# A two-layer encoder step on one core: the chunk loop of the delta-rule mixer written out as a software pipeline, and a third raw buffer for an expert table

## The chip, the core and the metric

The kernel runs on one core of one Trainium2 chip. The metric is device microseconds of one execution, the median of several runs. TensorE (PE in the profile), VectorE (DVE), ScalarE (ACT), GpSimdE (POOL) and SyncE (SP, which here only issues DMAs) each run their own list of instructions in order and meet through semaphores.

## The reference

Two streams, a prompt of 512 positions and a decode of 32, go through two layers in float32. The part of a layer that the change touches most is the RWKV-7 group, a recurrence over time on a 64x64 matrix state for each of eight heads:

```python
def step(S, inp):
    r_t, w_t, k_t, v_t, a_t, b_t = inp
    sa = jnp.einsum('bhij,bhj->bhi', S, a_t)
    S = S * w_t[:, :, None, :] + sa[..., None] * b_t[:, :, None, :] + v_t[..., None] * k_t[:, :, None, :]
    return S, jnp.einsum('bhij,bhj->bhi', S, r_t)
```

A layer also has an RG-LRU group (convolution and a scan), an output projection, a PEER expert layer, and a per-layer embedding. In the expert layer each of 8 heads picks 16 of 16,384 experts by product keys; `hid = xb . u[e]` and `out = sum gelu(hid) gate v[e]`. The outputs are the activations and the states after each stream. Prompt and decode have states of their own: the prompt's starts at zero, the decode's is an input.

## The kernel before

The two layers run one after the other, each as a chain of stages: input projection with the RG-LRU work inside it, RWKV preparation, **the chunk loop**, output projection, query projection, **the u phase** of the expert layer, its v phase, embedding.

**The chunk loop.** The recurrence is done in chunks of C = 64 positions: eight of the prompt and one (DEC0, 32 positions padded) of the decode, NCHUNK = 9. A chunk turns the recurrence into matrix products. TensorE makes the products of the scaled keys `s.bk` and queries `s.ar` (`products`, L733 ff., 8 matmuls, then 8 transposes through `ident`); DVE masks them (`first`, `second`); the triangular system is inverted by doubling in six levels (`level_y` L749, `level_x` L758 on TensorE, one ACT copy `s.ys` between them, and a mask and an add on DVE for each level); `right_side` (L773) applies the incoming state `st`; `finish` (L785) solves, makes the state's update and the outputs; DVE's `carry` (L1601) adds the update into `st` and decays it. Each group of eight matmuls appears as 16 records of 64x64x64 in the trace. Everything of a chunk that does not read `st` is independent of the chunk before it.

Two slots (`Slot(0)`, `Slot(1)`) hold the buffers and four PSUM banks each. A hardware loop (`Fori`, four passes) takes two neighbouring chunks at a time, and both slots go through the same step at about the same time: products of slot 0 and slot 1, then level by level 0, 1, 0, 1. Slot 0's right side is placed after level 1, slot 1's only after slot 0's `finish` and `carry`, for it needs the state. Only when both carries are done are the `tilde` operations for the next two chunks run on DVE (L1561). The decode chunk is run last, alone, after the loop; DVE first saves the prompt's state to `stp` and puts the decode's state into `st`. `passed` adds a semaphore increment behind most waits.

**The u phase.** 128 tiles of the u table (`in_ut`, 512 KB each) are loaded by SP in two halves (`load_u`, L499) into one of two raw buffers `uraw`. ACT copies a half to a rounded high part `uh` (`high_u`, L1190), DVE subtracts to the low part `ul` (`low_u`, L1790), and `hidden` (L873) on TensorE multiplies high and low parts with the activations. SP waits before a load until DVE has read the same half two tiles earlier (`ul_ready`). In DVE's list the tiles are taken in 64 pairs: 8 head pairs, then three blocks of ten `route` pairs (top-k, many DVE operations) and eight `hot` pairs (one-hot gate matrices), then two pairs. Between them go row gathers by POOL, their dot products on DVE (`weigh_row`, L1806), saves of the activations (`expert_inputs`) and of the gate matrix by ACT's DMA queue.

**Constants.** `cn` holds constants in SBUF for the whole run, loaded once: identity, masks, then `eye` (64 columns), `level` (384), `reset` (580) and `fold`.

Of the kernel before, what the change touches and what calls it, by code (L numbers as in the profile page):

```python
# [85 lines left out]
NUG = 5  # L86
NV = 4
# [3 lines left out]
assert PART <= PAIRS_U and HOT_PAIRS * 4 == GB  # L91

# [57 lines left out]
def trunk(nc, x, p, small, const, spread, mixw, wkv0, w_in, w_out, wq, keys, ut, u, v, wple, y, small_out, wkv_out):  # L150
    ctx = ExitStack()
    with ctx:
# [30 lines left out]
        sm = take(NSM)  # L183
        cn = take(NCN)
# [51 lines left out]
        class Slot:  # L236


            def __init__(self, i):
# [4 lines left out]
                self.ar = take(NT * P).rearrange("p (m t) -> p m t", m=NT)  # L244
# [40 lines left out]
        uraw = [take(KD * P).rearrange("p (k n) -> p k n", k=KD) for _ in range(2)]  # L285
        uh_at = aligned(top[0])
# [84 lines left out]
        nsp_ready = sem("nsp_ready")  # L371
# [13 lines left out]
        state_ready = sem("state_ready")  # L385
# [19 lines left out]
        u_in = [[sem(f"u_in{i}{half}") for half in range(2)] for i in range(2)]  # L405
# [13 lines left out]
        eos_out, accg_out = sem("eos_out"), sem("accg_out")  # L419
# [12 lines left out]
        waits_passed = {e.engine: sem(f"waits_passed{i}") for i, e in enumerate([nc.sync, nc.tensor, nc.vector, nc.scalar])}  # L432

# [6 lines left out]
        def passed(eng):  # L440


            eng.sem_inc(waits_passed[eng.engine], 1)
# [12 lines left out]
        def _(sp_):  # L456
# [17 lines left out]
            for L in range(DEPTH):  # L474
# [43 lines left out]
                for m in range(2, NK):  # L518
# [96 lines left out]
        def _(pe):  # L615
# [53 lines left out]
            for L in range(DEPTH):  # L669
# [59 lines left out]
                pe.wait_ge(cum_ready, L + 1)  # L729

                def products(s, k):
# [8 lines left out]
                    last.then_inc(s.pair_done, 1)  # L740
                    for m in range(NT):
                        nc.tensor.transpose(ps[:, s.bank + 2, m * P:(m + 1) * P], s.bk[:, m, :], ident)
# [4 lines left out]
                def level_y(s, k, lv):  # L747

                    n = L * s.per + k  # L749
                    if lv == 0:  # L750
                        pe.wait_ge(s.turn_out, n + 1)
                    pe.wait_ge(s.m_ready, n * (LEVELS + 1) + lv + 1)
                    passed(pe)
# [5 lines left out]
                def level_x(s, k, lv):  # L759
                    pe.wait_ge(s.y_out, (L * s.per + k) * (LEVELS - 1) + lv)  # L760
                    passed(pe)
# [9 lines left out]
                def right_side(s, k):  # L771

                    pe.wait_ge(s.gm_ready, L * s.per + k + 1)  # L773
                    if s.i == 1:
                        pe.wait_ge(state_ready, L * s.per + k + 1)
                    passed(pe)
                    for m, q in PAIRS:
                        hd = 2 * m + q // HD
                        mm(s.psum(0)[q:q + C, m, :], s.ar[:, m, 0:C], st[:, m, q:q + HD], start=True, stop=False)
# [4 lines left out]
                def finish(s, k):  # L784
# [4 lines left out]
                    passed(pe)  # L789
# [3 lines left out]
                    pe.wait_ge(s.sa_out, n + 1)  # L793
                    passed(pe)
# [4 lines left out]
                    for m in range(NT):  # L799
                        mm(s.psum(0)[:, m, :], st[:, m, :], s.ar[:, m, C:P], start=True, stop=False)  # L800
# [6 lines left out]
                def chunks(k, work):  # L807

                    for s in work:
                        products(s, k)  # L810
                    for lv in range(LEVELS):
                        for s in work:
                            level_y(s, k, lv)
                        if lv > 0:
                            for s in work:
                                level_x(s, k, lv)
                        if lv == 1:
                            right_side(slots[0], k)
                    for s in work:
                        if s.i == 1:  # L820
                            right_side(s, k)
                        finish(s, k)

                passed(pe)
# [140 lines left out]
                pe.wait_ge(accg_out, L + 1)  # L965
                back(acc_g, 6)
                for t in range(NB):
                    pe.wait_ge(eos_out, L * NB + t + 1)
                    back(eos[t], 2 * t)
# [27 lines left out]
        def _(act):  # L997
# [28 lines left out]
            for L in range(DEPTH):  # L1026
# [13 lines left out]
                act.wait_ge(lam_step, 2 * L + 1)  # L1040
# [6 lines left out]
                def lru_tanh(ns):  # L1047
                    act.wait_ge(nsp_ready, L + 1)
# [15 lines left out]
                for n in range(2, IN_T):  # L1064
                    high_weight(L, 0, n, wh1)
                    if n == 2:
                        act.wait_ge(lam_step, 2 * L + 2)
# [52 lines left out]
                def values(s, col):  # L1120

# [3 lines left out]
                def turned(s, k):  # L1125
                    act.wait_ge(s.turn_done, L * s.per + k + 1)
                    av(s.bkT, ps[:, s.bank + 2, :], ACT.Copy)
                    av(s.sav, ps[:, s.bank + 3, :], ACT.Copy).then_inc(s.turn_out, 1)

                def level(s, k, lv):  # L1130
# [3 lines left out]
                def right_side(s, k):  # L1134
# [3 lines left out]
                def finish(s, k, col):  # L1138
                    n = L * s.per + k
                    act.wait_ge(s.sa_done, n + 1)  # L1140
# [4 lines left out]
                    act.wait_ge(s.step_done, n + 1)  # L1145
                    passed(act)
                    av(o[:, :, col], s.psum(0), ACT.Copy).then_inc(o_out, 1)

                def chunks(k, work, col):
                    for s in work:  # L1150
                        values(s, col(s))
                    for s in work:
                        turned(s, k)
                    for lv in range(1, LEVELS):
                        for s in work:
                            level(s, k, lv)
                        if lv == 1:
                            right_side(slots[0], k)
                    for s in work:
                        if s.i == 1:  # L1160
                            right_side(s, k)
                        finish(s, k, col(s))

                with act.Fori(0, NCH // 2) as k:
                    chunks(k, slots, lambda s: bass.ds(k * (2 * C) + s.i * C, C))
                chunks(NCH // 2, slots[:1], lambda s: slice(DEC0, DEC0 + C))
# [24 lines left out]
                def high_u(m, half):  # L1191
                    i = L * NK + m
                    act.wait_ge(u_in[m % 2][half], 16 * (i // 2 + 1))
# [808 lines left out]
```

## Time and profile before

| | |
|---|---|
| median of 3 runs | 4164.2 us (4155.7 to 4173.1) |
| the profiled execution | 4173.6 us, of which the span in the trace is 4171.8 us |
| mean granted TensorE clock | 0.933 of full |
| PE busy | 3686.5 us (88%) |
| DVE busy | 2972.4 us (71%) |
| ACT, POOL busy | 1655.2 us (40%), 922.7 us (22%) |
| chunk loop, layer 0 and layer 1 | 216.5 to 455 us, 2289 to 2523.5 us |
| u phase, layer 0 | about 665 to 1447 us |
| v phase, layer 0 | about 1453 to 1987 us |

Busy time is instruction time of an engine; matmuls are pipelined, and a busy PE isn't at its peak. The clock column of a window is the TensorE clock granted, where 1.00 is 2.4 GHz and 0.50 is 1.2 GHz. In the chain of waits each row is a start, a length and the work that the end of the run waited for in that time; "issue" is time for which the profile shows nothing, often a semaphore on its way.

### The profile page before, as it was taken

Reading aid. Unit: us, or ns where it says so; the run is one execution under the profiler, and the core shown is the slowest. Engines: PE = TensorE matmul, PEld = TensorE weight load, DVE = VectorE, ACT = ScalarE, POOL = GpSimd, SP = SyncE. Lnnn points to the kernel's source line nnn. Section 1 sums busy time; section 2 is a strip of 40 time slices with the busy share of each in tenths; the row PEclk is TensorE's granted clock in tenths of the full one; section 3 lists DMA queues with packets and bytes.
Section 4 is the critical chain, followed back from the end, with each engine's and each line's share of the span. In section 5 each row is a group of like instructions: output and inputs, shape, how many; then the busy total and the mean of one; then the engine's idle time right before and its main releaser. Section 6 shows DMA issues by size and latency. Waiting matters only on the chain.

```text
span 4171.8 us, 65717 instructions
## 1 busy us (share of the span) xinstructions
PE 3686.5 (88%) x24642; PEld 3310.0 (79%) x24642; DVE 2972.4 (71%) x6046; ACT 1655.2 (40%) x3067; POOL 922.7 (22%) x742
## 2 busy tenths in 40 slices
PE   8877798889898799999888777979998997999998
PEld 8766597889898688888787666978888886888877
DVE  5845325988989598888367542279898895888882
ACT  4312022366666633333233210223847575333331
POOL 3200031222222233333031000302222232333320
PEclk9977799999999899999999877999999998999999
DMA  3100023669898999998221000247798989999972
GB/s 119 50 1 0 19 81 129 233 232 314 280 310 282 296 394 380 379 380 330 75 80 42 1 0 28 82 136 251 255 322 268 313 270 319 390 379 380 380 279 64
DMA packets 544480, 888.94 MB, mean 213 GB/s; under 512 B 37808, under 2 KB 361936, under 8 KB 543440
## 3 DMA queue, kind: packets, MB, share of 16 engines
q1 hardware_dynamic: 311728, 444.32, 30.3%
q0 software_dynamic: 92416, 336.17, 23.1%
q10 hardware_dynamic: 140064, 104.88, 7.9%
q8 instruction: 164, 2.69, 0.3%
q14 instruction: 108, 0.88, 0.1%
HBM read 777.55 MB, written 107.67 MB: 212 GB/s over the span
## 4 chain that ended last, share of the span: by engine, by line
PE 62%; DVE 21%; DMA 5%; ACT 5%; issue 3%; ACTq 2%; DVEq 2%; SPq 0%
PE ps L955 26%; PE ps L647 10%; PE ps L631 7%; PE ps L879 5%; DMA m<-in_ut 4%; DVE m L1795 3%; PE ps L916 3%; DVE m L1806 3%; PE ps L882 2%; ACT m L1231 1%; ACTq L1249 1%; DMA expert_inputs<-m 1%; PE ps L623 1%; PE ps L755 1%; PE ps L763 1%
## 5 line engine op out<-in xcount | busy, mean ns | idle before, releaser
L955 PE MATMUL ps<-m,m 128*128 128x512 f32 x4608 | 1066.9, 394 | 11.9 <-DVE m L1867 11.9
L955 PEld LDWEIGHTS ps<-m,m 128*128 128x128 f32 x4608 | 867.2, 188 | 211.3 <-issue 12.4
L879 PE MATMUL ps<-m,m 128*128 128x384 f32 x4096 | 846.5, 349 | 53.6 <-ACT m L1204 53.1
L879 PEld LDWEIGHTS ps<-m,m 128*128 128x128 f32 x4096 | 737.6, 196 | 58.6 <-ACT m L1204 56.8
L608 POOL DMA_INDIRECT m<-in_u,m x320 | 352.2, 1101 | 1128.3 <-DVE m L1806 927.3
L882 PE MATMUL ps<-m,m 128*128 128x384 f32 x2048 | 465.0, 350 | 135.4 <-DVE m L1795 135.1
L1197 ACT ACTIVATE m<-m 128x512 fp32r<-128x512 f32 x512 | 319.3, 625 | 590.9 <-DMA m<-in_ut 473.3
L608 POOL DMA_INDIRECT m<-in_v,m x320 | 359.5, 1124 | 786.0 <-DVE ps L1879 554.0
L1303 ACT ACTIVATE m<-m 128x1024 fp32r<-128x1024 f32 x256 | 271.5, 1061 | 651.3 <-PE ps L955 648.1
L882 PEld LDWEIGHTS ps<-m,m 128*128 128x128 f32 x2048 | 376.6, 197 | 155.2 <-DVE m L1795 155.2
L647 PE MATMUL ps<-m,m 128*128 128x272 f32 x3648 | 469.0, 290 | 5.5 <-ACT m L1021 4.6
L647 PEld LDWEIGHTS ps<-m,m 128*128 128x128 f32 x3648 | 463.6, 190 | 9.0 <-issue 5.4
L1795 DVE TENSOR_TENSOR m<-m,m 128x512 fp32r<-128x512 f32 x512 | 332.9, 688 | 96.6 <-ACT m L1197 94.4
L580 POOL TENSOR_TENSOR m<-m,m 128x1024 fp32r<-128x1024 f32 x76 | 191.6, 2523 | 629.9 <-ACT m L1021 629.9
L1879 DVE SCALAR_TENSOR_TENSOR ps<-m,m,ps 128x1024 f32<-128x1024 f32 x254 | 326.2, 1284 | 4.6
L1852 DVE TENSOR_TENSOR m<-m,m 128x1024 fp32r<-128x1024 f32 x256 | 312.1, 1219 | 14.3 <-ACT m L1303 14.3
L1806 DVE CUSTOM_DVE_ANT_0 m<-m,ps 128x1024 f32<-128x1024 f32 x256 | 306.4, 1217 | 6.5 <-issue 0.5
L631 PE MATMUL ps<-m,m 128*128 128x272 f32 x1152 | 275.1, 401 | 39.2 <-DVE m L1664 20.6
L631 PEld LDWEIGHTS ps<-m,m 128*128 128x128 f32 x1152 | 223.6, 195 | 87.5 <-DVE m L1664 21.5
L1817 DVE TENSOR_SCALAR m<-m,m 128x128 f32<-128x128 f32 x768 | 213.2, 348 | 79.2 <-PE ps L916 56.4
L1231 ACT ACTIVATE m<-m,m 128x128 f32<-128x128 f32 x768 | 243.8, 392 | 0.5
L916 PE MATMUL ps<-m,m 128*128 128x128 f32 x1536 | 207.4, 278 | 17.7 <-DVE m L1817 13.8
(264 smaller groups left out, 4009.5 us busy)
## 6 DMA issues: line engine op xcount, KB each, us to landing
m<-in_ut SPq DMA_DIRECT2D x512, 256.0 KB, 5.1
m<-in_v SPq DMA_DIRECT2D x256, 512.0 KB, 6.3
expert_inputs<-m ACTq DMA_DIRECT2D x256, 192.0 KB, 3.7
gate_matrix<-m ACTq DMA_DIRECT2D x48, 1024.0 KB, 9.7
m<-gate_matrix SPq DMA_DIRECT2D x256, 192.0 KB, 5.2
m<-expert_inputs SPq DMA_DIRECT2D x256, 192.0 KB, 7.2
m<-in_w_in SPq DMA_DIRECT2D x44, 512.0 KB, 3.8
m<-in_wq SPq DMA_DIRECT2D x32, 512.0 KB, 3.9
```

The lines of the kernel that those rows point to most:

```text
L608: pool.indirect_dma_start(ug[r % NUG], None, table[:, :], bass.IndirectOffsetOnAxis(ap=index.bitcast(U32), axis=0)).then_inc(row_in[r % NU ...
L631: last = mm(ps[:, bank + a, 0:HALF], wslot[:, slot, k, :], rhs[:, n, a * HALF:(a + 1) * HALF], start=(n == 0), stop=(n == len(ks) - 1))
L647: last = mm(ps[:, 2 * j + a, 0:HALF], lhs[j][:, k, :], rhs[:, k, a * HALF:(a + 1) * HALF], start=(k + w == 0), stop=(k == KD - 1 and w == 2))
L879: mm(ps[:, j, 0:DT], uh[j][:, k, :], x_[:, k, :], start=(k == 0 and x_ is xh), stop=False)
L882: last = mm(ps[:, j, 0:DT], ul[j][:, k, :], xh[:, k, :], start=False, stop=(k == KD - 1))
L916: last = mm(ps[:, 4 + s, j * P:(j + 1) * P], oneA[:, s, j, :], oneB[:, s, j, :], start=True, stop=True)
L955: last = mm(ps[:, 2 * t + a, :], lhs[s][:, t * BLK:(t + 1) * BLK], rhs[s][:, a * 512:(a + 1) * 512], start=(n + w == 0), stop=(n == NK - 1 ...
L1197: av(uh[m % 2][:, ks, :], uraw[m % 2][:, ks, :], ACT.Copy).then_inc(uh_ready, 1)
L1795: tt(ul[m % 2][:, ks, :], uraw[m % 2][:, ks, :], uh[m % 2][:, ks, :].bitcast(F32), ALU.subtract).then_inc(ul_ready, 1)
L1806: nc.vector.tensor_tensor_reduce(row, row, other, 1.0, 0.0, ALU.mult, ALU.add, at).then_inc(row_used, 1)
L1852: tt(vl[n % NV], vraw[n % NV], vh[n % NV].bitcast(F32), ALU.subtract).then_inc(vl_ready, 1)
L1879: last = stt(acc, row, w, acc, ALU.mult, ALU.add)
```

## The change

The two `Fori` loops on TensorE, ACT and DVE are gone. All nine chunks are written out, p = 0 to 8, with p = 0 the decode chunk; chunk p uses slot p % 2. One step of the written-out loop holds the first half of chunk p ("new") and the second half of chunk p - 1 ("old"), interleaved group by group. `products` is cut into `pairs`, `turn_keys` and `turn_values`; `finish` into `solve` and `step`; `tilde` into `tilde_keys` and `tilde`. The queries `s.ar` get a second buffer per slot (in the place of the mixer weights `mw`). `carry(p - 2)` opens DVE's step p. The `tilde` work for chunk p + 1 is in step p. `pairs` and `right_side` wait for two different semaphores of the carry: `state_read` after its PSUM reads and `state_ready` at its end. The decode's state is put into `st` before the loop; after `carry(0)` it is saved to `sts` and `st` is cleared.

```diff
-                passed(pe)
-                with pe.Fori(0, NCH // 2) as k:
-                    chunks(k, slots)
-                chunks(NCH // 2, slots[:1])
...
+                def pairs(p):
+                    s, k = turn_of(p)
                     n = L * s.per + k
                     pe.wait_ge(s.tilde_ready, n + 1)
-                    pe.wait_ge(s.v_ready, n + 1)
-                    passed(pe)
+                    if p > 1:
+                        pe.wait_ge(state_read, L * NCHUNK + p - 1)
+                        pe.wait_ge(o_out, L * NCHUNK + p - 1)
                     for m, q in PAIRS:
-                        last = mm(ps[:, s.bank + q // HD, m * P:(m + 1) * P], s.bk[q:q + HD, m, :], s.ar[q:q + HD, m, :],
+                        last = mm(ps[:, s.bank + q // HD, m * P:(m + 1) * P], s.bk[q:q + HD, m, :], s.ar[k % 2][q:q + HD, m, :],
                                   start=True, stop=True)
                     last.then_inc(s.pair_done, 1)
...
+                for p in range(NCHUNK + 1):
+                    new, old = p < NCHUNK, p > 0
+                    if new:
+                        pairs(p)
+                    if old:
+                        level_y(p - 1, 3)
+                    if new:
+                        turn_keys(p)
+                    if old:
+                        level_x(p - 1, 3)
+                    if new:
+                        turn_values(p)
+                    if old:
+                        level_y(p - 1, 4)
+                        right_side(p - 1)
+                        level_x(p - 1, 4)
+                    if new:
+                        level_y(p, 0)
+                    if old:
+                        level_y(p - 1, 5)
+                    if new:
+                        level_y(p, 1)
+                    if old:
+                        level_x(p - 1, 5)
+                    if new:
+                        level_x(p, 1)
+                    if old:
+                        solve(p - 1)
+                    if new:
+                        level_y(p, 2)
+                    if old:
+                        step(p - 1)
+                    if new:
+                        level_x(p, 2)
...
+                def carry(p):
+                    s, k = turn_of(p)
+                    end = cols_of(p).stop - 1
                     dve.wait_ge(s.step_done, L * s.per + k + 1)
                     for q in (0, HD):
                         at = st[q:q + HD, :, q:q + HD]
-                        tt(at, s.psum(1)[q:q + HD], at, ALU.add)
+                        last = tt(at, s.psum(1)[q:q + HD], at, ALU.add)
+                    last.then_inc(state_read, 1)
                     dve.drain()
                     for q in (0, HD):
                         at = st[q:q + HD, :, q:q + HD]
-                        tt(at, at, TB[1][q:q + HD, :, end].to_broadcast([HD, NT, HD]), ALU.mult)
-                    dve.drain()
-
-                def chunks(k, work, col, end):
-                    for s in work:
-                        tilde(s, col(s))
-                    for s in work:
-                        first(s, k)
-                    for s in work:
-                        second(s, k)
-                    dve.drain()
-                    for lv in range(1, LEVELS):
-                        for s in work:
-                            level(s, k, lv)
-                    for s in work:
-                        carry(s, k, end(s))
-                        if s.i == 0 and len(work) == 2:
-                            dve.sem_inc(state_ready, 1)
-
-                with dve.Fori(0, NCH // 2) as k:
-                    chunks(k, slots, lambda s: bass.ds(k * (2 * C) + s.i * C, C),
-                           lambda s: bass.ds(k * (2 * C) + (s.i * C + C - 1), 1))
-                dve.wait_ge(wkv_in, L * 16 + 16)
+                        last = tt(at, at, TB[1][q:q + HD, :, end:end + 1].to_broadcast([HD, NT, HD]), ALU.mult)
+                    if p == 0:
+                        dve.drain()
+                        for q in (0, HD):
+                            copy(sts[q:q + HD, :, :], st[q:q + HD, :, q:q + HD])
+                        dve.drain()
+                        last = dve.memset(st[:, :, :], 0.0)
+                    last.then_inc(state_ready, 1)
+                    dve.drain()
...
+                for p in range(NCHUNK + 1):
+                    new, old = p < NCHUNK, p > 0
+                    if p > 1:
+                        carry(p - 2)
+                    if new:
+                        first(p)
+                    if old:
+                        level(p - 1, 3)
+                    if new:
+                        first_inverse(p)
+                    if old:
+                        level(p - 1, 4)
+                    if new:
+                        second(p)
+                    if p + 1 < NCHUNK:
+                        tilde_keys(p + 1)
+                    if old:
+                        level(p - 1, 5)
+                    if new:
+                        level(p, 1)
+                        masked(p)
+                    if p + 1 < NCHUNK:
+                        tilde(p + 1)
+                    if new:
+                        level(p, 2)
+                carry(NCHUNK - 1)
...
+                for p in range(NCHUNK + 1):
+                    new, old = p < NCHUNK, p > 0
+                    if old:
+                        level(p - 1, 3)
+                    if new:
+                        turned_keys(p)
+                    if old:
+                        level(p - 1, 4)
+                    if new:
+                        turned_values(p)
+                    if old:
+                        right_side(p - 1)
+                    if p + 1 < NCHUNK:
+                        values(p + 1)
+                    if old:
+                        level(p - 1, 5)
+                    if new:
+                        level(p, 1)
+                    if old:
+                        solved(p - 1)
+                    if new:
+                        level(p, 2)
+                    if old:
+                        stepped(p - 1)
```

Of the three loops the first is TensorE's, the second DVE's, the third ACT's. On DVE `tilde_keys(0)` and `tilde(0)` come before the loop and `carry(NCHUNK - 1)` after it.

The u phase gets NU = 3 raw buffers. The third lies over `eye`, `level` and `reset` of `cn`; SP loads these constants again at the start of layer 0's v phase, and DVE and TensorE wait for them in layer 1.

```diff
-                        if m > 1:
-                            sp_.wait_ge(ul_ready, 2 * (i - 2) + half + 1)
-                        sp_.dma_start(uraw[m % 2][:, ks, :], ut[L, m][:, ks, :]).then_inc(u_in[m % 2][half], 16)
+                        if m >= NU:
+                            sp_.wait_ge(ul_ready, 2 * (i - NU) + half + 1)
+                        sp_.dma_start(uraw[m % NU][:, ks, :], ut[L, m][:, ks, :]).then_inc(u_in[m % NU][half], 16)
...
+                load_u(2)
+                for m in range(3, NK):
...
                 load_v(0)
                 load_v(1)
+                if L + 1 < DEPTH:
+                    back = slice(CN["eye"], CN["eye"] + D)
+                    sp_.dma_start(cn[:, back], const[:, back]).then_inc(const_in, 16)
```

`passed` and its semaphores are dropped, and a few semaphores are joined (`nsp_ready` into `lam_step`, `accg_out` and `eos_out` into `sums_out`), with the same order of work.

## Rows read from the trace of the kernel before

**Rows 1.** The page: the span, and the shares of the chain that ended last.
```profile
span 4171.8 us, 65717 instructions
...
PE 62%; DVE 21%; DMA 5%; ACT 5%; issue 3%; ACTq 2%; DVEq 2%; SPq 0%
```

**Rows 2.** Windows over both chunk loops: us, busy us of engines (instructions), clock, DMA, GB/s.
```profile
216.46:455.00 238.54, 172.45 (x3169) 152.37 (x3169) 112.07 (x253) 47.89 (x114) 0.00 (x0) 0.74 0.00 1
2289.00:2523.50 234.50, 169.17 (x3169) 149.69 (x3169) 111.58 (x253) 47.89 (x114) 0.00 (x0) 0.76 0.00 1
```

**Rows 3.** Chain of waits, first two chunks of layer 0: start us, us, what.
```profile
221.58 2.08 PE ps L738 x16
...
225.55 1.12 PE ps L738 x16
...
242.41 0.68 PE ps L755 x16
243.09 0.47 PE ps L763 x16
...
244.92 1.11 issue
...
249.04 0.52 PE ps L791 x16
...
250.50 0.69 PE ps L797 x16
...
254.26 2.07 issue
...
261.06 1.12 PE ps L797 x16
...
266.36 0.42 DVE m L1606
...
271.18 2.08 PE ps L738 x16
```

**Rows 4.** Chain of waits, the decode chunk of layer 0, alone.
```profile
416.29 2.08 PE ps L738 x16
...
432.42 1.13 PE ps L755 x16
...
434.10 1.12 PE ps L763 x16
...
454.90 7.17 PE ps L655 x16
```

**Rows 5.** Groups by line on DVE, chunk loop of layer 0: busy us, mean ns | idle before.
```profile
L1597 DVE TENSOR_TENSOR m<-ps,m 128x512 f32<-128x512 f32 x36 | 24.8, 689 | 36.3 <-PE ps L767 35.9
L1571 DVE TENSOR_TENSOR m<-m,m 128x256 f32<-128x256 f32 x54 | 22.6, 419 | 1.1
...
L1606 DVE TENSOR_TENSOR m<-ps,m 64x256 f32<-64x256 f32 x18 | 7.6, 422 | 65.4 <-PE ps L803 65.3
```

**Rows 6.** Windows of 2 us around the first two chunks.
```profile
252.00:254.00 2.00, 2.00 (x18) 1.56 (x17) 0.00 (x0) 0.00 (x0) 0.00 (x0) 0.70 0.00 0
254.00:256.00 2.00, 0.26 (x4) 0.07 (x2) 1.49 (x4) 0.38 (x1) 0.00 (x0) 0.50 0.00 0
...
276.00:278.00 2.00, 2.00 (x22) 1.72 (x21) 0.88 (x3) 0.28 (x1) 0.00 (x0) 0.83 0.00 0
```

**Rows 7.** A window of 10 us in the second pass of the loop.
```profile
286.00:296.00 10.00, 9.16 (x276) 8.58 (x273) 5.54 (x11) 2.19 (x7) 0.00 (x0) 1.00 0.00 0
```

**Rows 8.** Waits of the whole run: us in total, times, longest us.
```profile
DVE m L1795 <- ACT m L1197: 94.4, 40, 26.8
```

**Rows 9.** Windows over the second route stretch and the hot stretch behind it.
```profile
985.00:1098.00 113.00, 94.60 (x506) 90.91 (x506) 100.76 (x290) 39.36 (x73) 23.63 (x21) 0.95 0.96 316
...
1098.00:1195.00 97.00, 95.13 (x636) 92.86 (x635) 87.18 (x219) 94.78 (x230) 29.62 (x30) 1.00 0.82 271
```

**Rows 10.** The page: DMA issues, KB each, median us to landing.
```profile
m<-in_v SPq DMA_DIRECT2D x256, 512.0 KB, 6.3
```

More of the change, by code:

```diff
@@ L86 @@
 NUG = 5
+NU = 3
 NV = 4
@@ L91, with u_loads @@
 assert PART <= PAIRS_U and HOT_PAIRS * 4 == GB
+def u_loads(L, m):
+    return L * len(range(m % NU, NK, NU)) + m // NU + 1
 def place(p):
@@ L183, in trunk @@
         sm = take(NSM)
+        cn_at = aligned(top[0])
         cn = take(NCN)
@@ L243, in __init__ @@
                 self.bk = take(NT * P).rearrange("p (m t) -> p m t", m=NT)
-                self.ar = take(NT * P).rearrange("p (m t) -> p m t", m=NT)
+                self.ar = [take(NT * P, at).rearrange("p (m t) -> p m t", m=NT) for at in (None, mw_at + i * NT * P)]
                 self.vc = take(NT * P).rearrange("p (m t) -> p m t", m=NT)
@@ L285, in trunk @@
         uraw = [take(KD * P).rearrange("p (k n) -> p k n", k=KD) for _ in range(2)]
+        assert CN["level"] + LEVELS * C == CN["reset"] and MW + LEVELS * C + C >= D
+        uraw.append(take(D, cn_at + CN["eye"]).rearrange("p (k n) -> p k n", k=KD))
         uh_at = aligned(top[0])
@@ L384, in trunk @@
         cum_ready, exp_ready = sem("cum_ready"), sem("exp_ready")
-        state_ready = sem("state_ready")
+        state_read, state_ready = sem("state_read"), sem("state_ready")
         o_out = sem("o_out")
@@ L404, in trunk @@
         gate_saved = [sem(f"gate_saved{i}") for i in range(4)]
-        u_in = [[sem(f"u_in{i}{half}") for half in range(2)] for i in range(2)]
+        u_in = [[sem(f"u_in{i}{half}") for half in range(2)] for i in range(NU)]
         v_in = [sem(f"v_in{i}") for i in range(NV)]
@@ L438, in trunk, with turn_of, cols_of @@
         v_rows = v.rearrange("l e d -> (l e) d")
-        def passed(eng):
-            eng.sem_inc(waits_passed[eng.engine], 1)
+        def turn_of(p):
+            return slots[p % 2], p // 2
+        def cols_of(p):
+            return slice(DEC0, DEC0 + C) if p == 0 else slice((p - 1) * C, p * C)
         def halves(bank, w):
@@ L757, in level_y, with level_x @@
                     last.then_inc(s.y_done, 1)
-                def level_x(s, k, lv):
+                def level_x(p, lv):
+                    s, k = turn_of(p)
                     pe.wait_ge(s.y_out, (L * s.per + k) * (LEVELS - 1) + lv)
-                    passed(pe)
                     for m, q in PAIRS:
@@ L782, in right_side, with solve @@
                     last.then_inc(s.f_done, 1)
-                def finish(s, k):
+                def solve(p):
+                    s, k = turn_of(p)
                     n = L * s.per + k
@@ L792, in finish, with step @@
                     last.then_inc(s.sa_done, 1)
-                    pe.wait_ge(s.sa_out, n + 1)
-                    passed(pe)
+                def step(p):
+                    s, k = turn_of(p)
+                    pe.wait_ge(s.sa_out, L * s.per + k + 1)
                     for m, q in PAIRS:
@@ L1144, in finish, with stepped @@
                     last.then_inc(s.sa_out, 1)
[L1145 to L1149, printed above, removed]
-                    for s in work:
-                        values(s, col(s))
-                    for s in work:
-                        turned(s, k)
-                    for lv in range(1, LEVELS):
-                        for s in work:
-                            level(s, k, lv)
[L1157 to L1166, printed above, removed]
+                def stepped(p):
+                    s, k = turn_of(p)
+                    act.wait_ge(s.step_done, L * s.per + k + 1)
+                    av(o[:, :, cols_of(p)], s.psum(0), ACT.Copy).then_inc(o_out, 1)
+                act.wait_ge(cum_ready, L + 1)
+                values(0)
+                for p in range(NCHUNK + 1):
[22 more added lines that the diff above has]
+                        stepped(p - 1)
                 act.wait_ge(wide_done, wide_of(L, "var"))
@@ L1192, in high_u @@
                     i = L * NK + m
-                    act.wait_ge(u_in[m % 2][half], 16 * (i // 2 + 1))
+                    act.wait_ge(u_in[m % NU][half], 16 * u_loads(L, m))
                     if m > 1:
@@ L1559, in _, with tilde_keys @@
                 eyes = eye.unsqueeze(1).to_broadcast([P, NT, C])
-                def tilde(s, col):
+                def tilde_keys(p):
+                    s, k = turn_of(p)
+                    col = cols_of(p)
+                    if k > 0:
+                        dve.wait_ge(s.turn_done, 2 * (L * s.per + k))
                     for q, (b_at, k_at) in ((0, (0, C)), (HD, (C, 0))):
@@ L1590, in second, with level @@
                     last.then_inc(s.gm_ready, 1)
-                def level(s, k, lv):
+                def level(p, lv):
+                    s, k = turn_of(p)
                     if lv + 1 < LEVELS:
@@ L1599, in level @@
                         tt(s.xt, s.psum(3, NT * C), s.xt, ALU.add).then_inc(s.m_ready, 1)
-                def carry(s, k, end):
+                def carry(p):
+                    s, k = turn_of(p)
+                    end = cols_of(p).stop - 1
                     dve.wait_ge(s.step_done, L * s.per + k + 1)
@@ new lines, in carry @@
+                    last.then_inc(state_ready, 1)
+                    dve.drain()
+                tilde_keys(0)
+                tilde(0)
+                for p in range(NCHUNK + 1):
[23 more added lines that the diff above has]
+                        level(p, 2)
@@ L1633, in _ @@
+                carry(NCHUNK - 1)
                 for q in (0, HD):
                     copy(stp[q:q + HD, :, :], st[q:q + HD, :, q:q + HD])
-                dve.drain()
-                for q in (0, HD):
-                    copy(st[q:q + HD, :, q:q + HD], sts[q:q + HD, :, :])
-                chunks(NCH // 2, slots[:1], lambda s: slice(DEC0, DEC0 + C), lambda s: slice(DEC0 + C - 1, DEC0 + C))
-                for q in (0, HD):
-                    copy(sts[q:q + HD, :, :], st[q:q + HD, :, q:q + HD])
```

123 lines of the change are left out of this document (65 added, 58 removed).

## The prediction

> **What bounds the kernel now.** I read the page's chain first: over the 4171.8 us span PE ends 62% of it and DVE 21% [rows 1], so a stage is worth something only where one of these two, or the way between them, shortens. The profiled execution took 4173.6 us (1.8 around the span), 9.4 over the median of 4164.2; I sum against the former and take 9.4 off at the end.
>
> Then the windows of the stage that is changed. The chunk loop takes 238.5 and 234.5 us, 11% of the span together. No engine fills it: PE 172 busy of 238.5, DVE 112, ACT 48, and PE's clock is 0.74 [rows 2]. So it is bound by hand-offs and by the clock. The chain shows both. In a fast stretch eight matmuls of a level take 0.68 to their end, the next eight are issued 0.47 after the last [rows 3]. One pass of two chunks runs from 221.58 to 271.18, 49.6 us, and its second half is poor: solve, two ACT copies (249.56 to 250.50), step (3.76, to 254.26), 2.07 until the carry is through, and then all again for the other slot at half clock, where a step takes 5.3 (261.06 to 266.36) [rows 3]. The carry, tilde and the next products follow one after the other until 271.18. The decode chunk alone goes from 416.29 to 454.90, 38.6 us [rows 4].
>
> The clock by rows: it is 0.70 in 252 to 254 and 0.50 after it, when PE has been busy 0.26 of 2 us, and 0.83 in 276 to 278 [rows 6]. The first products of a pass run at half clock (2.08), the second slot's, 4.0 us of unbroken matmuls later, at full (1.12) [rows 3]. With two slots level on level PE is busy 9.16 of 10 us and the clock stays at 1.00 [rows 7].
>
> **The chunk loop, step by step.** In the new loop a step holds one chunk's work. I lay it out at full clock from t = 0, where the old chunk's `step` has been issued. `level_x(new, 2)`: 2 x 0.47, done at 1.15. DVE adds it (0.69, [rows 5]): 1.9. Carry's first two operations (2 x 0.42, [rows 5]): 2.8. Only then may `pairs` start, for it waits for `state_read`: 2.95 to 4.05 (1.12, [rows 3]). Behind that wait on PE's queue stand all groups of the next step, level 3 of the older chunk among them, so the wait is a hole of 1.8 us that nothing fills. Then y3 and the four key transposes (half of a pair group, an estimate) to 5.0; x3 waits for ACT's copy, 5.3 to 6.25; value transposes to 6.75; y4 waits for DVE's add, 7.3 to 7.8; right side (16 matmuls, 0.94 and its tail) to 8.95; x4 to 9.9; y0 to 10.4; y5 after mask and add (0.42 + 0.69) 11.0 to 11.5; y1 to 11.95; x5 12.25 to 12.7; x1 to 13.7; solve to 14.2; y2 after DVE's add 14.8 to 15.3, which hides the two ACT copies; step 3.76 to 19.1. DVE's own work in a step (112.07 / 9 = 12.5 us, [rows 2]) fits beside this, and carry's second half, 1.9 to 3.75 in all, is over long before the right side needs the state. `tilde`, gone from the path, lies where DVE waits for PE.
>
> So a step takes **19.1 at full clock**, against 24.8 for a chunk of a pass now. At half clock the same list has 24.4 of PE work (pairs 1.9, transposes 1.7, six y 5.1, x 7.65, right side 1.9, solve 0.85, step 5.3; a group of eight issues in 0.85, 1.12 to its end, [rows 3, 4]) and 2.8 of holes: **27.2**.
>
> Which clock? A step's end is like what it is now: a hole before `step`, then `step`, then 1.8 of nothing, and there the clock fell [rows 6]. Behind `pairs` come 4 us of nearly unbroken work, after which it rose [rows 3]. So I take it low from about 0 to 7 of each step, which adds 0.96 for pairs, 0.4 for y3, 0.35 for transposes, 0.4 for half of x3 and 0.3 at the edges: **21.5**.
>
> The ends: step 0 has only the new chunk, 11 at full and 14 at half clock (416.29 to 432.42 less the right side, [rows 4]): 12.5. Step 1 has no carry to wait for: 19.5. Steps 2 to 8: 7 x 21.5 = 150.5. Saving the decode's state and clearing `st` in step 2: 1.2. The last step has only the old chunk: at half clock 432.42 to 454.90 and the right side, 24.4 with carry and copies [rows 4]; at full 18.2; taken 21.3. Sum 205.0. Now, from first products to the stage's end, it is 233.3 (221.58 to 454.90, [rows 3, 4]), and 229.4 in layer 1 (4 shorter, [rows 2]). That saves 28.3 + 24.4 = **52.7**. All at full clock it would be 11 + 17.3 + 133.7 + 1.2 + 18.2 = 181.4, saving 99.9; all at half 255.4, losing 48.1.
>
> Dropping `passed` removes an increment per wait, and the loops' address arithmetic goes: taken as nothing beside the 0.14 that a hand-off takes. The decode state's copy into `st` is now before the loop, under PE's bonus matmuls that DVE waits for anyway; the cost if that cover were gone is under 1 us.
>
> **The third raw buffer.** A load may start one tile earlier. What it can give is DVE's wait for ACT's high copies, 94.4 in 40 times; two of 26.8 are behind the gate saves at the phase's end and stay [rows 8]. That leaves 40.8 in both layers as the most, and part of it is ACT behind the activation saves. In the hot stretches PE is the bound (95.13 of 97) and nothing is gained. In the route stretches DVE is (100.76 of 113), with the DMA engines 0.95 busy at 316 GB/s [rows 9], so an earlier load mostly queues longer. I take 8. From below: the same bytes, each no later, but they may push gathers and saves back by a few us; I keep -5 to 40.8.
>
> The DMA share of 0.95 in that stretch is measured [rows 9]. The Trainium skill, "DMA: Bandwidth & Descriptors", section "Issuing engines are not separate DMA queues", says that DMAs from SP, ACT and GpSimd run on the same 16 engines and interleave; by that rule an earlier load there takes bandwidth from gathers and saves, and this term would be 0 and the sum 8 higher.
>
> **Loading the constants again.** Once, 512 KB among the gate saves and v loads at the end of layer 0's u phase: a transfer of that size lands in 6.3 [rows 10], and at 316 GB/s [rows 9] it takes 1.7 of the engines. It stands ahead of the first gate loads on SP's queue: 1.4 taken, 0 to 6.3. The constants are needed some 800 us later.
>
> **Sum.** 4173.6 - 52.7 - 8 + 1.4 = 4114.3; less 9.4: **4105**.
>
> **Rivals.**
> *The clock stays up.* Old and new groups alternate, PE has 14.4 of work in 19.1, and the hole is 1.8 instead of 2.07 and nearly 5 (266.4 to 271.2, [rows 3]) in a pass. Against it: the fall already in 252 to 254 [rows 6], during a step, before any hole of 2 us. 4173.6 - 99.9 - 6.6 = 4067; less 9.4: 4058.
> *The clock stays down* (the slower side). The single chunk, whose matmul groups wait for ACT and DVE one by one, ran at half clock, y at 1.13 and x at 1.12 [rows 4]. If a step's holes keep it there for the whole loop, the step is 27.2 and the loop 255.4: 4173.6 + 48.1 - 6.6 = 4215; less 9.4: 4206. It decides from a step of 25.3 on, where the loop is as long as now. Against it: at half clock PE would be busy 24.4 of 27.2, and such work raised the clock each pass.
> *The step does not overlap as laid out*, no change. Written-out code is read once; the first pass shows a hole of 1.11 in which PE waited for nothing that the profile shows [rows 3]. Three such holes in a step, or as much from groups that stand behind one wait in three lists, make it 24.8, which takes back 7 x 3.3 in a layer and some in the ends, all 52.7: 4167; less 9.4: 4158. Against it: no other hole of that kind is among these rows, and 24.8 is a pass without any of the overlap.
>
> **Chances.** Forecast 0.55, clock up 0.20, no overlap 0.15, clock down 0.10. Within 0.5% (4143 to 4185) is about what a measurement of this kernel can't tell from no change; the first two cases are faster than that, the third is within, the fourth slower. Range: from between the first rival and the forecast's own low end with the whole 40.8 of the u phase, 4045, to the third rival with no gain from loads, 4165; the forecast's own range is 4070 to 4140 (steps of 19.8 to 23).
>
> **What would show it.** Forecast: loops of about 205 us a layer, first products to the mean's matmuls, clock 0.75 to 0.85 in them, products of neighbouring chunks 21 to 22 apart, a hole of about 1.8 before each. Clock up: 19 apart, 0.95 and more. Clock down: 27 apart, 0.5. No overlap: about 25, with holes that the list above doesn't have. For the buffer, DVE's wait for high copies would fall from 94.4 towards 55, and the route windows from 113. I am wrong if steps are under 19 or over 25, or if the u phase moves by more than 20 a layer.

## The result and the profile after

The changed kernel takes **4027.8 us** (median of 4 runs, 4024.6 to 4031.2); the kernel before, run beside it, 4168.7. The ratio is 0.966 (95% interval 0.9645 to 0.9675). The forecast was 4105, and the range ended at 4045: the direction is right, the gain is more than twice the one forecast, and the time lies below the range.

The profiled execution took 4028.2 us, against 4173.6 before; the spans in the traces differ by 145.3. Two stages hold nearly all of it, in both layers:

| stage (layer 0 / layer 1), us | before | after | saved |
|---|---|---|---|
| chunk loop, first products to the mean's matmuls | 233.3 / 229.7 | 177.8 / 176.2 | 55.5 + 53.5 = 109.0 |
| u phase, end of the query projection to the first v matmul | 791.0 / 791.3 | 774.9 / 774.4 | 16.1 + 16.9 = 33.0 |

That is 142.0; the other 3.3 is spread. The page of after, its span and its chain's shares [rows 1]:

```profile
span 4026.4 us, 65006 instructions
...
PE 67%; DVE 19%; ACT 4%; DMA 3%; issue 3%; ACTq 2%; DVEq 1%; SPq 0%
```

PE ends 67% of the span instead of 62; the shares of DVE and DMA fell by two points each. Windows over both chunk loops of after, in the columns of [rows 2]:

```profile
222.90:400.80 177.90, 149.24 (x3169) 129.30 (x3169) 106.53 (x242) 48.82 (x116) 0.00 (x0) 0.93 0.01 2
2220.30:2396.50 176.20, 147.46 (x3168) 128.08 (x3169) 106.52 (x242) 48.76 (x116) 0.00 (x0) 0.95 0.01 2
```

PE's granted clock in the loop went from 0.74 and 0.76 to 0.93 and 0.95, and for the same 3169 matmuls PE was busy 149 us instead of 172 in layer 0. ACT's work is what it was. Now the chain of waits of after, layer 0 (start, us, what; L753 are the products, as L738 was before [rows 3]; L778 and L786 are `level_y` and `level_x`, L822 is the first part of `step`):

```profile
222.98 2.08 PE ps L753 x16
...
233.57 1.09 PE ps L753 x16
...
268.39 1.60 issue
269.99 1.16 PE ps L753 x16
...
282.16 0.62 PE ps L822 x16
285.30 0.61 PE ps L786 x16
...
286.38 1.60 issue
287.98 1.89 PE ps L753 x16
289.87 1.05 PE ps L778 x16
...
305.88 1.60 issue
307.49 1.16 PE ps L753 x16
...
323.87 1.60 issue
325.48 1.86 PE ps L753 x16
```

From the third chunk on, a hole of 1.60, in which PE does nothing, stands before each products group. Products are 18.0 apart (269.99 to 287.98) or 19.5 (287.98 to 307.49), in turn: behind every second hole the products take 1.8 to 1.9 instead of 1.16 and the next level (L778) 1.05 instead of 0.61. The windows of 2 us of after (columns as in [rows 6]) show the clock there:

```profile
268.00:270.00 2.00, 0.40 (x15) 0.29 (x12) 1.46 (x4) 0.00 (x0) 0.00 (x0) 1.00 0.00 0
...
286.00:288.00 2.00, 0.40 (x16) 0.29 (x11) 1.47 (x4) 0.00 (x0) 0.00 (x0) 1.00 0.00 0
288.00:290.00 2.00, 2.00 (x20) 1.77 (x22) 0.90 (x3) 0.00 (x0) 0.00 (x0) 0.55 0.00 0
290.00:292.00 2.00, 2.00 (x26) 1.65 (x26) 1.51 (x4) 0.49 (x2) 0.00 (x0) 0.59 0.00 0
292.00:294.00 2.00, 1.80 (x44) 1.49 (x42) 0.92 (x2) 0.50 (x1) 0.00 (x0) 1.00 0.05 12
```

Two holes alike (PE busy 0.40 of 2 us): after the first the clock stays at 1.00, after the second it is 0.55 and 0.59 in the next two windows, in which PE is busy all the time, and then back at 1.00.

The u phase. Waits of the whole run of after (us in total, times, longest), to set against [rows 8]:

```profile
ACT m L1255 <- PE ps L920: 270.7, 120, 6.7
...
DVE m L1887 <- ACT m L1255: 81.0, 25, 27.3
...
ACT m L1255 <- DMA m<-in_ut: 15.9, 7, 4.1
```

L1255 is ACT's high copy of a u tile (L1197 before). It now waits for PE to give back the buffer that it writes, and hardly any more for the load (15.9). Before, the load was the wait:

```profile
ACT m L1197 <- DMA m<-in_ut: 473.3, 193, 7.9
```

The wait on which the prediction rested, DVE's for the high copies, fell from 94.4 to 81.0 only. The gain stands elsewhere. Windows of the phase's first stretch (head and first route) and of the whole second route stretch in the kernel before, columns as in [rows 2]:

```profile
662.20:884.20 222.00, 179.14 (x976) 172.93 (x975) 194.86 (x610) 75.06 (x128) 31.86 (x29) 0.92 0.60 201
...
982.30:1098.10 115.80, 97.40 (x526) 93.70 (x525) 103.50 (x295) 42.08 (x79) 24.68 (x22) 0.96 0.96 316
```

The same two stretches of after, and 500 us of its v phase:

```profile
605.60:818.20 212.60, 179.29 (x972) 173.59 (x972) 194.50 (x610) 75.56 (x128) 32.08 (x29) 0.92 0.61 208
...
915.50:1026.90 111.40, 95.60 (x518) 92.48 (x517) 102.32 (x294) 40.59 (x77) 24.89 (x22) 0.95 0.96 324
...
1400.00:1900.00 500.00, 500.00 (x2170) 406.80 (x2169) 444.97 (x515) 177.58 (x242) 166.95 (x149) 1.00 1.00 378
```

With the same DVE work the first stretch is 9.4 shorter: DVE idles 18.1 instead of 27.1. That is more than half of the layer's 16.1, and it lies where the DMA engines are busy 0.60 of the time. The second route is 4.4 shorter: the DMA engines are at 0.96 before and after, and move 324 GB/s instead of 316. A wait within the first stretch of the kernel before:

```profile
DVE m L1722 <- ACT m L1213: 13.4, 2, 9.9
```

The same wait in the first stretch of after:

```profile
DVE m L1814 <- ACT m L1271: 8.4, 2, 6.5
```

DVE's wait for ACT's copies of the scores (L1722, now L1814) is 5.0 shorter. These copies stand in ACT's list behind high copies, and so behind u loads; the prediction's row did not hold this wait. The chain shows where it comes from. At the start of the phase the kernel before has two tiles in its buffers and waits for the load of the third:

```profile
662.24 0.44 DVE m L1677
...
665.10 6.53 DMA m<-in_ut
...
675.57 1.07 DVE m L1722 x5
```

In after that load was issued ahead (at 600.60; in the kernel before at 665.10), and no DMA stands on the chain there:

```profile
605.65 0.44 DVE m L1769
...
615.60 1.07 DVE m L1814 x5
```

From DVE's first operation of the phase to L1722 it is 13.33 before, and to L1814 9.95 after: 3.4 of the 9.4 come from this one wait at the phase's start.

### The profile page after: what moved, and what is told of

Its sections match the earlier page's. It is cut to its first block, busy times and chain, and to the rows that moved or that the text cites. A ratio compares the mean times of both kernels' runs of the same rounds, so it can differ in the third digit from the quotient of the medians.

```text
span 4026.4 us, 65006 instructions
## 1 busy us (share of the span) xinstructions
PE 3629.5 (90%) x24642; PEld 3255.2 (81%) x24642; DVE 2970.4 (74%) x6048; ACT 1654.1 (41%) x3067; POOL 923.9 (23%) x742
## 4 chain that ended last, share of the span: by engine, by line
PE 67%; DVE 19%; ACT 4%; DMA 3%; issue 3%; ACTq 2%; DVEq 1%; SPq 0%
PE ps L993 26%; PE ps L659 10%; PE ps L643 7%; PE ps L917 6%; PE ps L920 3%; PE ps L954 3%; DVE m L1887 3%; DMA expert_inputs<-m 3%; DVE m L1898 2%; ACT m L1289 2%; PE ps L778 1%; PE ps L786 1%; ACTq L1307 1%; PE ps L635 1%; DVE m L1677 1%
## 5 line engine op out<-in xcount | busy, mean ns | idle before, releaser
L1255 ACT ACTIVATE m<-m 128x512 fp32r<-128x512 f32 x512 | 318.6, 624 | 374.8 <-PE ps L920 270.7
L643 PEld LDWEIGHTS ps<-m,m 128*128 128x128 f32 x1152 | 223.3, 194 | 87.4 <-DVE m L1756 21.5
L1262 ACT ACTIVATE m<-ps 128x384 f32<-128x384 f32 x256 | 123.8, 484 | 259.1 <-PE ps L920 183.7
```

Of the source, the lines that this page charges most:

```text
L643: last = mm(ps[:, bank + a, 0:HALF], wslot[:, slot, k, :], rhs[:, n, a * HALF:(a + 1) * HALF], start=(n == 0), stop=(n == len(ks) - 1))
L1255: av(uh[m % 2][:, ks, :], uraw[m % NU][:, ks, :], ACT.Copy).then_inc(uh_ready, 1)
```

## Experiments

**Which part gave what.** Changed kernel with two raw buffers (e1), and the kernel before with three and only what the third needs, the constants loaded again and the waits for them (e2).

```diff
# e1, of the changed kernel          # e2, of the kernel before
-NU = 3                              +NU = 3
+NU = 2                              +uraw.append(take(D, cn_at + CN["eye"])...)
                                     ...
```

> The changed kernel with two raw buffers for u (the constants are still loaded again). The two changes add up: the u phase, 775 us from the end of the query projection to the first matmul of the v phase, goes back to 791 in each layer and the chunk loops stay at 178 us: 4028 + 33 = about 4061. Rival: the longer u phase of before came from something else in the change (semaphores, the state in which the phase starts) and the buffer gives the 8 that I had put down: about 4036.

Measured: 4061.3, ratio to before 0.9748 (0.9724 to 0.9772); u phase 792.0 and 790.2.

> The kernel before with the third raw buffer alone. If the buffer gives 16.5 us a layer: the u phase at 775, chunk loops at 233 and 229, about 4169 - 33 = 4136. Rival (the term of the prediction): 8 in all, about 4160.

Measured: 4134.6, ratio 0.9928 (0.9902 to 0.9953); u phase 771.4 and 770.5 against 791.0 and 791.3.

The first theory held in both. The loop alone gives 106.6, the buffer alone 33.2, together 139.8 of the 140.9 between the medians: the two parts add, as far as these times can tell. In e1 ACT's wait for the load is back, in the row where before had 473.3, and DVE's for the high copy nearly so; the wait for the third tile at the phase's start is back too (6.54 at 608.23):

```profile
ACT m L1255 <- DMA m<-in_ut: 492.9, 208, 7.0
...
DVE m L1887 <- ACT m L1255: 89.5, 39, 27.9
```

**Is it the writing out?** The kernel before with its chunk loop as straight code, its order kept (the same on ACT and DVE).

```diff
-                with pe.Fori(0, NCH // 2) as k:
+                for k in range(NCH // 2):
...
```

> The kernel before with its hardware loops written out and the order of the work unchanged (two slots level on level, decode chunk last). If the order and the clock that it keeps make the gain: passes of 48 to 50 us, 0.74 clock, about 4160 to 4169, no more than 1 us a pass from the loops' address arithmetic. Rival: the written-out code itself (no branch, constant addresses) carries a large part of the 108 us that the two chunk loops lost: under 4130.

Measured: 4155.4, ratio 0.9969 (0.9957 to 0.9982), some 12 us; passes of layer 0 still take 48 to 49 (269.03 to 316.81), each with its first products at 2.08. So the rival is out: about a tenth of the loop's gain comes with straight code, a little more than expected, and the rest is from the order. In the trace (of a run of 4165.2, the slowest of the ten) the eight passes are 1.8 shorter in all: 193.5 and 190.5 a layer against 194.7 and 191.2. The one large difference is the decode chunk of layer 1. In e3 (columns as in [rows 2]):

```profile
2486.26:2517.78 31.52, 19.95 (x353) 17.23 (x353) 10.53 (x23) 5.82 (x12) 0.00 (x0) 0.82 0.01 2
```

In the kernel before:

```profile
2485.00:2523.49 38.49, 26.93 (x353) 23.51 (x353) 10.53 (x23) 5.82 (x12) 0.00 (x0) 0.54 0.01 1
```

It is 7.0 shorter at a higher clock; in layer 0 the same chunk had 0.50 in e3 and was not shorter. So what the loops' own control costs is not shown beyond the 1.8. The Trainium skill, "Runtime: NRT & Kernel Launch", section "Instruction fetch mechanics", says that a taken branch can stall the fetch and that unrolled code is preferred for it; the direction agrees with this run, which doesn't show a single stall.

**Does the hole pull the clock down?** Three kernels with another length of the hole: the carry moved from the head of the next step to before the last add of the same step (e4, no hole before the products; `level` is cut into its mask and its add for it), and four or eight memsets in front of the carry (e5, e6; they write a tile that is written again later).

```diff
# e4
-                    if p > 1:
-                        carry(p - 2)
...
                     if new:
-                        level(p, 2)
-                carry(NCHUNK - 1)
+                        level_mask(p, 2)
+                    if old:
+                        carry(p - 1)
+                    if new:
+                        level_add(p, 2)
...
# e5 (e6: range(8)), in carry, ahead of the two adds
+                    for _ in range(4):
+                        dve.memset(stp[:, :, :], 0.0)
+                        dve.drain()
```

> The changed kernel with the carry moved on DVE from the head of the next step to before the last add of the same step, so that the products need not wait for both. If the hole before the products (1.60 us, each step) is on the path and is what drops the clock in every second step: hole near 0, y3 and first 1.3 us earlier, steps of 16.7 all at full clock instead of 18.0 and 19.5 in turn, 14 us a layer: about 4000. Rival: the clock falls from the step's own matmuls: 16.7 and 18.2 in turn, 9 to 10 us a layer, about 4009. Second rival: the add that now waits behind the carry makes up for it, y3 is as late as before: 4028.

Measured: 4014.4, ratio 0.9634 (0.961 to 0.9658). The chain of e4 (L828 is the end of `step`, L1694 the carry, L1679 a level's add, L778 here level 3 of the older chunk):

```profile
265.41 0.29 PE ps L828 x4
265.72 0.42 DVE m L1694
...
267.61 0.70 DVE m L1679
268.36 0.68 PE ps L778 x16
...
285.26 0.68 PE ps L778 x16
```

From the third chunk on no products group is on the chain; they run at a clock of 1.00 beside the carry, and steps are 16.9 (268.36 to 285.26), in both layers the clock seldom falling. But level 3 now waits 2.66 (265.70 to 268.36), for both halves of the carry and the add. So the clock did what the first theory says, and the step is 0.2 over its 16.7; the time all the same lies 14 over its 4000, between the two rivals' 4009 and 4028. Of the 14 us a layer that it counted, layer 0 shows 7.0: five steps, not seven, are shorter, by 1.8 each, and the end, from level 3 of the last chunk on, takes 2.5 more than in the changed kernel (369.76 to 391.42 against 381.69 to 400.80), in part at a low clock (its `level_x` at 370.93 takes 1.12).

> The changed kernel with four memsets of a buffer that is not yet in use (about 0.33 us each with their drains) put on DVE ahead of each carry, which lengthens the hole before the products from 1.6 to about 2.9 us. If the hole is what drops the clock: it falls in every step, products at 1.8 to 2.1 and not at 1.16, steps of 18.0 + 1.3 + 1.5 = 20.8 against a mean of 18.75 now, 7 x 2.05 = 14 us a layer and one more at the end: about 4059. Rival (the fall is the step's own matmuls, whatever the hole): falls in every second step as now, steps of 20.0 in the mean, 9 to 10 a layer: about 4048.

Measured: 4078.9, ratio 0.9786 (0.9769 to 0.9802).

> The same with eight memsets, a hole of about 4.2 us. If the hole drops the clock: every step, and longer, steps of 18.0 + 2.6 + 2 to 2.4 = about 22.8, near the 21.5 that I had forecast for a hole of 1.8: 28 us a layer, about 4086. Rival: every second step, 18.75 + 2.6 = 21.4, 18.5 a layer: about 4067.

Measured: 4115.0, ratio 0.987 (0.9853 to 0.9886). Both are slower than any theory had them, in part because a memset with its drain costs 0.43 (3.34 - 1.60, by four) and not the 0.33 assumed. The chain of e5, holes and products:

```profile
289.59 3.34 issue
292.93 2.08 PE ps L753 x16
...
311.90 3.34 issue
315.24 1.56 PE ps L753 x16
```

The chain of e6, the same pieces:

```profile
319.60 5.05 issue
324.65 2.08 PE ps L753 x16
```

Now the clock is low behind every hole, in both layers. What is left of a step without hole and at full clock is 18.0 - 1.60 = 16.4 (and e7 below has this step); what a step has beyond that and its hole is the clock's price:

| kernel | hole before products | clock falls | step | price of the clock |
|---|---|---|---|---|
| e4 | none | seldom | 16.9 | about 0 (the 0.5 is level 3's wait) |
| after | 1.60 | every second step | 18.0 or 19.5 | 0 or 1.5 |
| e5 | 3.34 | every step | 21.1 to 22.4, mean 21.5 | 1.8 |
| e6 | 5.05 | every step | 23.8 to 24.4 | 2.5 |

That the hole brings the clock down is shown by lengthening it (e5, e6) and by taking it away (e4), with the same matmuls. A longer hole makes the step longer too, and the runs don't tell these two apart. Why 1.60 is too long in every second step and not in each is not settled.

**The gain that is left.** e4 with the carry's second half (the decay) behind the step's last add, so that level 3 waits for less.

```diff
+                def carry_scale(p):
+                    end = cols_of(p).stop - 1
...
                     if new:
                         level_add(p, 2)
+                    if old:
+                        carry_scale(p - 1)
```

> The kernel with the carry first, and its second half (the decay of the state) put behind the level's add, so that level 3 of the next step no longer waits for it. In the run before level 3 started 2.66 us after the step's last matmul: carry 1.9, add 0.7. If that chain is what sets the step (16.9), it is now products and level 3 one after the other, some 0.7 to 0.9 shorter: steps of 16.1, 5 to 6 us a layer, 4014 - 11 = about 4003. Rival: the state is later for the right side, or PE is at its own work (14.4 us a step) elsewhere: 4014.

Measured: **3997.4**, ratio 0.9589 (0.9571 to 0.9606), clear of the changed kernel's 0.9645 to 0.9675. The chain of e7, one step apart (L786 is `level_x`, L1679 a level's add):

```profile
265.39 0.61 PE ps L786 x16
...
266.52 0.69 DVE m L1679
...
281.77 0.61 PE ps L786 x16
```

The step is 16.4 (265.39 to 281.77), and layer 0's loop takes 160.4, 17.4 less than in the changed kernel. That is the 1.60 hole and the clock's price gone, and level 3's wait of e4 with them: level 3 now follows the products without a gap (267.49).

**A try elsewhere.** e7 with the last eight saves of the gates issued by SP instead of ACT, since they stand ahead of ACT's work where the u phase ends.

```diff
# on SP
+                for q in range(3):
+                    save_gates(q)
                 load_v(0)
                 load_v(1)
+                for q in range(3, 8):
+                    save_gates(q)
...
# on ACT
-                    elif pair == PART - 1:
-                        for q in range(8):
-                            save_gates(NB - 1, q)
```

> The same, and the last block's eight gate saves issued by SP behind its last u load (three, then the first two v loads, then five) and not by ACT, where they stand for 26 us ahead of the last tiles' copies. If ACT's queue is what held the end of the u phase: the last four tiles overlap the saves, 12 to 20 us a layer: about 3970. Rival: the v phase starts when the saves have landed anyway, and its loads wait: no change, about 4003.

Measured: 3993.5, ratio 0.9583 (0.9567 to 0.9599), not to be told from e7. The chain of e8 at the stretch where it should have gained:

```profile
1336.70 4.97 SPq L557
...
1341.71 4.04 SPq L557
...
1356.96 4.73 DMA m<-expert_inputs
```

Saves of 3 to 5 us each (L557) now stand in SP's queue ahead of the loads that v needs: the wait changed its queue.

## Why the prediction was wrong, by its steps

*What bounds the kernel*, hand-offs and the clock in the chunk loop, was right, and the mechanism was: old and new groups alternate, the pass's second half is gone, and in front of the products stands a hole that nothing fills (1.8 forecast, 1.60 measured).

*The list of a step* was right in its order and too long by 1.1: at full clock it gave 19.1; measured 18.0 (269.99 to 287.98). Of the 1.1, 0.6 is `step`: its 3.76 was read from 250.50 to 254.26, and in the second part of that the clock was already 0.70 [rows 6]. At full clock the group takes 3.14 (282.16 to 285.30), and in the second pass of the kernel before 3.21 (299.41 to 302.62). The sum with all at full clock, 181.4 for layer 0, was therefore itself 3.6 over the 177.8 measured, with three falls in it. Step 0 was 12.5, measured 10.6; step 1 19.5, measured 17.9. The last step and the one before it were 21.5 + 21.3 = 42.8, measured 37.8 (362.98 to 400.80).

**"Which clock?" is the step that failed.** "So I take it low from about 0 to 7 of each step", 2.4 us, made 21.5. The clock fell in every second step only, for less than 4 us, at a price of 1.5: six steps took 111.5 (251.49 to 362.98), 18.6 each, and in them the clock cost 3.0 where 14.4 was taken. The argument carried over what [rows 6] show, a fall by hole of about 2 us, to a hole of 1.8, as if its length did not matter. It also took over a hole before `step`, which its own list fills with y2: PE idles there 0.33 (to 281.48). And the fall during `step` that it cites is one of the first pass; in the second, `step` ran at full clock to its end. In the kernel before a pass has several holes close together: solve, copies, step, 2.07, then the other slot's step and nearly 5 until the products. In the changed kernel one short hole stands alone between 16 us of dense work. (That the nearness of the holes is what counts is argued from these rows; no run tried it. That a longer hole costs more is shown.) The forecast's 21.5 is the step of e5, whose hole is 3.34. The rival *the clock stays up* said 99.9 saved in the loops; measured 109.0. It had 0.20 where the forecast had 0.55. Its own steps were 19.1 each, at no fall; measured are 18.0 and 19.5, so its mechanism was not quite this one either. By parts of layer 0 the loop's forecast was too long by 1.9 (step 0), 1.6 (step 1), 18.7 (six steps and the 1.2 for the decode's state) and 5.0 (the end): 27.2, the difference of 205.0 and 177.8. The 18.7 are 11.4 from the clock, 6.6 from the list and 0.7 from the decode's state, which cost 0.5.

**The third raw buffer** was mis-sized: 8 taken, 33.0 measured, inside its bounds (-5 to 40.8). Three readings failed. First, the DMA share of the second route stretch was read as full, so that an earlier load would queue longer. (The share in [rows 9] is 0.96; the 0.95 that the prediction names stands in the column of the clock.) It was not full: with the third buffer the stretch moved 324 GB/s instead of 316 and shrank, and in the v phase (1400 to 1900 us of after) the engines moved 378 GB/s at a share of 1.00. The sentence of the Trainium skill drawn on there ("DMA: Bandwidth & Descriptors", section "Issuing engines are not separate DMA queues"), that DMAs of all issuers share 16 engines and interleave, is not contradicted, but the conclusion drawn from it, a term of 0, is refuted by e2 (0.9928, 0.9902 to 0.9953, from the buffer alone). Secondly, the first stretch was not looked at: its share is 0.60, and 9.4 of layer 0's 16.1 came there, 3.4 of them from the third tile's load at the start. Thirdly, DVE's wait for high copies was taken as all that a late load costs. ACT's own wait, 473.3, sends its lateness on to what ACT does behind it, as the wait for the copies of the scores shows. The bound of 40.8 was therefore no ceiling for the right reason: 13.4 came out of that row, the rest out of others, which these runs show only in part.

*Constants*: 1.4 taken; nothing of it stands on the chain. *Dropping `passed`* and the address arithmetic were taken as nothing; e3, which drops only the loops' control, shows 1.8 in the eight passes. No run drops `passed` alone.

The rivals *the clock stays down* and *no overlap* are out: no step is near 24.8 or 27.2, and no hole beyond the listed one is on the chain.

*The range.* With both uncertain terms at their better end the same sum gives 4173.6 - 99.9 - 40.8 + 1.4 - 9.4 = 4025. Measured 4027.8. That it comes so near is in part luck: the loops gave 9.1 more and the buffer 7.8 less. The range's low end, 4045, took no case with both good ends; the two parts add, as e1 and e2 show, so both could come, and nearly did.

## What to carry to other kernels

Price a clock fall by the hole that stands in front of it, in the new order: one hole of 1.60 us in an 18 us step dropped the clock in every second step here, one of 3.34 in every step, and moving four short DVE operations to another place in their list so that matmuls fill the hole was worth 30 us of 4028. Take the length of a group for a full-clock sum from a stretch whose clock you have read: a `step` taken at 0.70 made each step 0.6 too long. A high busy share of the DMA engines doesn't say that another buffer is worth nothing: look at who waits for the load (473 us on ACT) and at what stands behind that instruction in its list, the start of the phase included. Where two uncertain terms are independent, carry both good ends into the range.

## What the hardware showed unexpectedly

The clock's answer to a hole that comes back in every step is graded: with 1.60 us it fell in every second step, with 3.34 and 5.05 in every step, and a longer hole cost more time at low clock as well (1.5 us in a step where it fell, then 1.8 and 2.5). And an engine that gets its clock back needs less time for the same work: PE's busy time for the loop's 3169 matmuls went from 172 us to 149, and to 142 in e7, whose clock there is 0.98.
